# Second layer's entry: the low part of the first weight chunk on GpSimd, VectorE's context additions behind the first modulation

## The chip, the cores and the metric

The kernel runs on one core of a Trainium2 chip, as one program that holds two layers of a network. The metric is the time of one execution in microseconds of the device, taken over several runs. The engines are TensorE (PE in the profile; its weight loads are PEld), VectorE (DVE), ScalarE (ACT), GpSimd (POOL) and SyncE (SP), which issues most of the loads.

## What is computed

256 latent tokens and 256 context tokens, each of width 1024, pass through two layers. The part of a layer that matters here is its entry:

```python
for l in range(DEPTH):
    hx = modulate(rmsnorm(x_lat, norm1_g[l]), sh1[:, None], sc1[:, None])
    hc = modulate(rmsnorm(x_ctx, norm1_g[l]), csh1, csc1)
    mix_x, mix_c = token_mixer(hx, hc, tabs, p, lam, lam_init, not last)   # begins with hx @ w_in[l]
    x_lat = x_lat + g1[:, None] * mix_x
    hx2 = modulate(rmsnorm(x_lat, norm2_g[l]), sh2[:, None], sc2[:, None])
    x_lat = x_lat + g2[:, None] * ec_moe(hx2, router_w[l], moe_w1[l], moe_w3[l], moe_w2[l])
    ...                                   # the same for x_ctx where the layer isn't the last
return rmsnorm(x_lat, final_g)
```

`token_mixer` projects the tokens by `w_in` and runs four mixers; `compute_lambda` gives the two exponentials of `diff_lambda` that the second mixer needs. `ec_moe` is a mixture of 16 experts. All is float32.

## The kernel before

**How the engines are ordered.** Each engine has its own program, written out by hand, and runs it strictly in order; semaphores join them. A `Signal` is a semaphore with a count for each layer, and `wait_ge(*signal.at(l, n))` waits for the n-th event of layer l. An instruction that waits holds all that stands behind it on its engine.

**Weight chunks.** `w_in` comes in chunks of 128 x 1024 through a ring of six slots in SBUF. TensorE multiplies in a rounded form of float32, three products for one: high weights by high tokens, high by low, low by high. So each chunk j needs two steps before TensorE can use it: `high(l, j)` on ScalarE (line 1768) rounds the slot into `wr[:, j % 2, 0]` and raises `w_hi`; `low(l, j)` on VectorE (line 2250) subtracts that from the slot into `wr[:, j % 2, 1]` and raises `w_lo`. The slot is then free for SyncE's next load, which waits for `w_lo`. `high` of chunk j, from the third on, also waits for `chunk_sum` of chunk j - 2, since `wr` holds two chunks. In the first layer four opening chunks have their low parts made by GpSimd (line 2170).

**The entry of the second layer.** The last pack of the first layer's experts ends with eight products on TensorE, one for each half row tile of `x`. `add_last` on VectorE (line 2386) adds each to `x`: four for the latent tokens, then four for the context tokens. ScalarE takes squares of the latent tiles (lines 1775, 1785, 1788), VectorE their means (lines 2332, 2336, 2341), GpSimd the inverse roots (`roots`, line 2139). `normalise` on VectorE (line 2347) scales the two latent tiles, TensorE turns them (lines 1146 and 1162), and `modulate(l, 4)` makes four parts of modulated tokens: parts 0 and 2 by ScalarE (line 1818), 1 and 3 by VectorE (line 2365). Each part is then rounded by ScalarE (`part_high`, line 1807, signal `h_hi`) and its low part is made by VectorE (`part_low`, line 2353, signal `h_lo`). VectorE's order is part 1, low 0, part 3, low 1, low 2, low 3. ScalarE's is part 0, high 0, part 2, high 1, high 2, high 3, and then `high(l, 1)`. The first two projection chunks feed the branch `su`; TensorE's first chunk waits for `w_lo` 1 and then, for every two of its eight row blocks, for one more `h_lo`. A chunk of the first kind is 24 matmuls of 256 columns.

**Behind it.** VectorE then multiplies and sums `diff_lambda` (lines 2454 and 2455, signal `lam_step`). ScalarE waits for that (line 1873, one exponential) and only behind it, in its program, stand `high(l, 2)`, a square of a context tile, the first `su` output (line 1900, a Gelu), `high(l, 3)` and so on. The tables of Exp and Gelu are loaded in between. GpSimd's program has `roots(2 * l, 0, 1)`, both halves of the norm (latent, then context), then the load of the position bias (`load_bias`).

Of the kernel before, what the change touches and what calls it, by code (L numbers as in the profile page):

```python
# [288 lines left out]
def build(nc, A, out):  # L289
    f32, f32r = mybir.dt.float32, mybir.dt.float32r  # L290
    ACT = mybir.ActivationFunctionType
    ALU = mybir.AluOpType
# [4 lines left out]
    with ctx:  # L297
        def sb(name, shape, dt=f32, where=ctx):
            return where.enter_context(nc.sbuf_tensor(name, shape, dt))

        def signal(name, *per_layer):
            return Signal(ctx.enter_context(nc.semaphore(name)), list(per_layer))
# [6 lines left out]
        ring = ring_par[:, 0:NSLOT * 1024].rearrange("p (a b) -> p a b", a=NSLOT)  # L309
# [31 lines left out]
        with ExitStack() as mixers:  # L341
            wr = sb("wr", [128, 2, 2, 1024], f32r, mixers)
# [178 lines left out]
        def norm_pair(nn, j):  # L521

            a, b = tile_order(nn)[2 * j:2 * j + 2]
            return slice(a, b + 1, b - a)

        NN = [2 * n for _, _, n in norms]
        sq_done = signal("sq_done", *NN)
        sq_half = signal("sq_half", 1, 1)
        mean_done = signal("mean_done", norms[0][2], 0, norms[2][2], 0, 2)
        rstd_done = signal("rstd_done", *[n for _, _, n in norms[:4]], 2)  # L530
        xn_ready = signal("xn_ready", *NN)
        xt_ready = signal("xt_ready", 8, 8)
# [5 lines left out]
        w_hi = signal("w_hi", NC_ALL, NC_ALL)  # L538
        w_lo = signal("w_lo", NC_ALL, NC_ALL)
# [4 lines left out]
        aux_sum = signal("aux_sum", *[sum(u["kind"] in AUX for u in us) for us, _ in WU])  # L544
        tile_sum = signal("tile_sum", *[max(u.get("sums", 0) for u in us) for us, _ in WU])
        w_act = signal("w_act", *[n["act"] for _, n in WU])
        w_dve = signal("w_dve", *[n["dve"] for _, n in WU])
        dve_step = counter("dve_step")
# [160 lines left out]
        items, item_at = [], {}  # L709
# [102 lines left out]
        def last_bank(j, h, s):  # L812

            return 2 * j + h if s == 0 else (6, 7, 4, 5)[2 * j + h]
# [1302 lines left out]
        def _(pool):  # L2117
# [8 lines left out]
            def load_bias(l):  # L2126

                pool.dma_start(nab_all[:, :], A["na_rpb"][l]).then_inc(bias_loaded, 16)
# [6 lines left out]
            def roots(nn, *which):  # L2135
                for s in which:
                    pool.wait_ge(*mean_done.at(nn, s + 1))
                    c = norm_pair(nn, s)
                    pool.tensor_tensor(rstd[:, c], ms[:, c], half[:, 0:2], ALU.pow).then_inc(rstd_done.sem, 1)
# [14 lines left out]
            for l in range(L):  # L2154
# [9 lines left out]
                if l == 0:  # L2164
                    roots(2 * l, 0, 1)
                    for i in range(OPEN):
                        slot, _ = item_at["open_w", 0, i]
                        cols_ = slice(i % 2 * 512, i % 2 * 512 + 512)
                        pool.wait_ge(*w_hi.at(0, i + 1))
                        pool.tensor_tensor(wr[:, :, 1, cols_], ring[:, slot, :].rearrange("p (q n) -> p q n", q=2),  # L2170
                                           wr[:, :, 0, cols_].bitcast(f32), ALU.subtract).then_inc(w_lo.sem, 1)
                    pool.wait_ge(*mod_ready.at(0, 1))
                    load_bias(l)
                else:
                    roots(2 * l, 0, 1)
                    load_bias(l)

                pool.wait_ge(*v_stats.at(l, 1))
# [56 lines left out]
        def _(dve):  # L2235
            steps = [0]

            def step(ins):

                steps[0] += 1  # L2240
                ins.then_inc(dve_step, 1)
                dve.wait_ge(dve_step, steps[0])

            def low(l, j):

                if j >= NC_ALL or (l == 0 and j < OPEN):
                    return
                slot, _ = item_at["chunk", l, j]
                dve.wait_ge(*w_hi.at(l, j + 1))
                nc.vector.tensor_tensor(wr[:, j % 2, 1, :], ring[:, slot, :], wr[:, j % 2, 0, :].bitcast(f32),  # L2250
                                        ALU.subtract).then_inc(w_lo.sem, 1)

# [77 lines left out]
            def mean_half(nn, layer):  # L2330
                dve.wait_ge(*sq_half.at(layer, 1))
                step(nc.vector.tensor_scalar(ms_half, ss_half, 1.0 / D, EPS, ALU.mult, ALU.add))

            def mean_rest(nn):
                dve.wait_ge(*sq_done.at(nn, 2))
                nc.vector.scalar_tensor_tensor(out=ms[:, 1:2], in0=ss[:, 1:2], scalar=1.0 / D, in1=ms_half,
                                               op0=ALU.mult, op1=ALU.add).then_inc(mean_done.sem, 1)

            def mean_first(nn):
                dve.wait_ge(*sq_done.at(nn, 1))  # L2340
                return nc.vector.tensor_scalar(ms[:, 0:1], ss[:, 0:1], 1.0 / D, EPS, ALU.mult, ALU.add)

            def normalise(nn, s, which=(0, 1)):
                dve.wait_ge(*rstd_done.at(nn, s + 1))
                for j in which:
                    m = tile_order(nn)[2 * s + j]
                    nc.vector.tensor_scalar(xn[:, at_tile(m), :], x[:, m, :], rstd[:, m:m + 1], None, ALU.mult)\
                        .then_inc(xn_ready.sem, 1)
# [22 lines left out]
            def modulate(l, upto):  # L2371

                dve.wait_ge(*mod_ready.at(*MODULATED[l]))
                for t in range(1, upto, 2):
                    part_modulated(l, t)
                    if t > 1:
                        part_low(l, t - 2)
                    part_low(l, t - 1)
                part_low(l, upto - 1)

            def add_last(l, places):

                for s, j, h in places:
                    dve.wait_ge(*comb_sum.at(l, 2 * NT[l] * (NP[l] - 1) + 4 * j + 2 * h + s + 1))
                    xs_ = x[:, 2 * s + j, h * 512:(h + 1) * 512]
                    nc.vector.tensor_tensor(xs_, xs_, PS[:, last_bank(j, h, s), :], ALU.add).then_inc(comb_x.sem, 1)
# [46 lines left out]
            for l in range(L):  # L2433
# [3 lines left out]
                if l:  # L2437
                    add_last(l - 1, ((0, 0, 0), (0, 0, 1), (0, 1, 0), (0, 1, 1)))
                    step(mean_first(2 * l))
                    mean_half(2 * l, l - 1)  # L2440
                    mean_rest(2 * l)
                    add_last(l - 1, ((1, 0, 0),))
                    normalise(2 * l, 0)
                    add_last(l - 1, ((1, 0, 1), (1, 1, 0), (1, 1, 1)))
                if l:
                    low(l, 0)
                if l:
                    modulate(l, 4)
                    low(l, 1)

                dve.wait_ge(par_loaded[l], 16)
                lp = par[:, P_LAM:P_LAM + 256].rearrange("p (a b c) -> p a b c", a=2, b=2)
# [13 lines left out]
                for u in units:  # L2466
                    if splits_here(u):
                        low(l, u["q"] + 2)
                        if l:
                            context_step(l, u["q"])  # L2470
                        mod_work(l, PLAN_Q, u["q"])
                        for a, k in BY_Q[l].get(u["q"], ()):
                            accumulate(l, a, k)
# [463 lines left out]
```

## Time and profile before

| | |
|---|---|
| three runs | 1964.48, 1964.16, 1960.62 us; median 1964.16 |
| the profiled execution | 1961.55 us, of which the profile's span is 1959.7 us |
| TensorE busy | 1828.0 us (93%) |
| VectorE busy | 815.6 us (42%) |
| ScalarE busy | 454.2 us (23%) |
| GpSimd busy | 123.3 us (6%) |
| bytes read from HBM | 561.99 MB, 287 GB/s over the span |
| granted TensorE clock, mean | 0.989 of full speed |

All times in the trace count from the start of the span. The second layer's entry lies near 1100 us of it. "Idle before" is the time for which an engine had nothing to run before the instruction, and the arrow names what released it. Rows of a timeline merge neighbouring instructions of one line; the second number is then the time from the first one's start to the last one's end. Neighbouring instructions on VectorE and ScalarE overlap a little: the next one starts some 0.07 to 0.1 us before the row of the last one ends.

### The profile page before, as it was taken

Reading aid. Unit: us, or ns where it says so; the run is one execution under the profiler, and the core shown is the slowest. Engines: PE = TensorE matmul, PEld = TensorE weight load, DVE = VectorE, ACT = ScalarE, POOL = GpSimd, SP = SyncE. Lnnn points to the kernel's source line nnn. Section 1 sums busy time; section 2 is a strip of 40 time slices with the busy share of each in tenths; the row PEclk is TensorE's granted clock in tenths of the full one; section 3 lists DMA queues with packets and bytes.
Section 4 is the critical chain, followed back from the end, with each engine's and each line's share of the span. In section 5 each row is a group of like instructions: output and inputs, shape, how many; then the busy total and the mean of one; then the engine's idle time right before and its main releaser. Section 6 shows DMA issues by size and latency. Waiting matters only on the chain. (4 is left out here: it accounts for less than half of the span.)

```text
span 1959.7 us, 26828 instructions
## 1 busy us (share of the span) xinstructions
PE 1828.0 (93%) x11196; PEld 1092.6 (56%) x11196; DVE 815.6 (42%) x1242; ACT 454.2 (23%) x802; POOL 123.3 (6%) x137
## 2 busy tenths in 40 slices
PE   7999999999999999999888999999999988878786
PEld 5888766677888533333323587877997322222222
DVE  2676654665854422222211468667655010101001
ACT  3322244443222300000000342345443000000001
POOL 1081000000000100000000044000000000000000
PEclk8999999999999999999999999999999999999999
DMA  9635411113747999999999766643589999999997
GB/s 338 224 101 179 137 62 58 54 65 108 257 150 317 368 402 426 426 426 429 428 429 424 288 204 227 212 153 108 174 279 359 407 428 428 429 427 428 428 427 310
DMA packets 91985, 564.60 MB, mean 288 GB/s; under 512 B 10012, under 2 KB 10152, under 8 KB 67816
## 3 DMA queue, kind: packets, MB, share of 16 engines
q1 hardware_dynamic: 90824, 556.60, 72.6%
q0 software_dynamic: 512, 4.40, 0.6%
q10 hardware_dynamic: 544, 2.10, 0.3%
q8 instruction: 79, 1.29, 0.3%
q14 instruction: 26, 0.21, 0.0%
HBM read 561.99 MB, written 1.06 MB: 287 GB/s over the span
## 5 line engine op out<-in xcount | busy, mean ns | idle before, releaser
L1062 PE MATMUL PS<-hTr,wr 128*128 128x512 f32 (+1 forms) x2688 | 518.0, 349 | 8.4 <-DVE hTr L2353 5.7
L1062 PEld LDWEIGHTS PS<-hTr,wr 128*128 128x128 f32 x2688 | 428.3, 191 | 75.7 <-issue 15.2
L1644 PE MATMUL PS<-arena 128*32 128x512 f32 x1536 | 285.3, 603 | 45.8 <-DMA arena<-in_moe_w 22.5
L2250 DVE TENSOR_TENSOR wr<-ring_par,wr 128x1024 fp32r<-128x1024 f32 x148 | 186.9, 1263 | 134.0 <-ACT wr L1768 133.4
L1768 ACT ACTIVATE wr<-ring_par 128x1024 fp32r<-128x1024 f32 x148 | 156.4, 1057 | 269.5 <-PE PS L1062 265.1
L1644 PEld LDWEIGHTS PS<-arena 128*32 128x32 f32 x1536 | 81.8, 111 | 234.1 <-issue 234.1
L1062 PE MATMUL PS<-wr,hTr 128*128 128x512 f32 x816 | 188.8, 391 | 0.9 <-DVE wr L2250 0.9
L2794 DVE TENSOR_TENSOR x_work<-x_work,PS 128x512 f32<-128x512 f32 x72 | 45.7, 683 | 329.8 <-PE PS L1062 329.8
L1062 PEld LDWEIGHTS PS<-wr,hTr 128*128 128x128 f32 x816 | 151.9, 188 | 34.3 <-DVE wr L2250 2.3
L1644 PE MATMUL PS<-e_h,arena 128*32 128x512 f32 x720 | 121.6, 599 | 15.2 <-DMA e_h<-in_moe_w 15.0
L1644 PE MATMUL PS<-e_wr,arena 128*32 128x512 f32 x416 | 128.6, 602 | 0.4 <-PE PS L1644 0.4
L1644 PE MATMUL PS<-arena,nab 128*32 128x512 f32 x480 | 114.4, 601 | 9.7 <-DMA e_wr<-in_moe_w 6.7
L2076 ACT ACTIVATE arena<-PS 128x512 f32<-128x512 f32 x24 | 13.0, 594 | 413.1 <-PE PS L1644 413.0
L2822 DVE TENSOR_TENSOR nab<-PS,arena 128x512 f32<-128x512 f32 x24 | 15.5, 686 | 213.3 <-PE PS L1644 213.3
L1644 PE MATMUL PS<-e_h,nab 128*32 128x512 f32 x608 | 92.3, 593 | 4.4 <-DMA e_h<-in_moe_w 3.8
L1644 PEld LDWEIGHTS PS<-e_h,arena 128*32 128x32 f32 x720 | 35.9, 111 | 86.6 <-issue 86.6
L2271 DVE SCALAR_TENSOR_TENSOR spare<-ring_par,cond,spare 128x1024 f32<-128x1024 f32 x63 | 80.9, 1312 | 1.3
L2640 DVE SCALAR_TENSOR_TENSOR x_work<-x_work,PS 128x512 f32<-128x512 f32 (+1 forms) x56 | 32.1, 573 | 115.7 <-PE PS L1062 115.7
L1644 PEld LDWEIGHTS PS<-arena,nab 128*32 128x32 f32 x480 | 30.2, 111 | 79.3 <-issue 77.4
L1946 ACT ACTIVATE x_work<-PS,small 128x512 f32<-128x512 f32 (+1 forms) x96 | 58.2, 613 | 69.7 <-DVE small L2576 69.3
L1644 PE MATMUL PS<-e_wr,nab 128*32 128x512 f32 x256 | 74.2, 609 | 0.0
L2006 ACT ACTIVATE x_work<-PS 128x512 f32<-128x512 f32 (+1 forms) x64 | 31.4, 491 | 177.1 <-PE PS L1062 177.1
(250 smaller groups left out, 1938.2 us busy)
## 6 DMA issues: line engine op xcount, KB each, us to landing
arena<-in_moe_w SPq DMA_DIRECT2D x72, 2048.0 KB, 17.3
e_h<-in_moe_w SPq DMA_DIRECT2D x42, 2048.0 KB, 18.3
ring_par<-in_w_in SPq DMA_DIRECT2D x136, 512.0 KB, 3.7
e_wr<-in_moe_w SPq DMA_DIRECT2D x24, 2048.0 KB, 20.4
ring_par<-in_w_mod SPq DMA_DIRECT2D x92, 512.0 KB, 4.5
ring_par<-in_w_br SPq DMA_DIRECT2D x64, 256.0 KB, 3.5
e_h<-in_moe_w SPq DMA_DIRECT2D x32, 512.0 KB, 14.0
arena<-in_moe_w SPq DMA_DIRECT2D x32, 512.0 KB, 6.2
```

Of the source, the lines that this page charges most:

```text
L1062: return nc.tensor.matmul(o, a, b, start=first, stop=last)
L1644: ins = nc.tensor.matmul(PS[r:r + CAP, bank + h, :], src[:, k, r:r + CAP], rows_in(l, 6 * G * at_ + n + g, p, kk)[:, h * 512:(h + 1) * 512 ...
L1768: nc.scalar.activation(wr[:, j % 2, 0, :], ring[:, slot, :], ACT.Copy).then_inc(w_hi.sem, 1)
L1946: ins = nc.scalar.activation(p_t[:, i_ % 2, a, 0:nk], PS[:, a, 0:nk], ACT.Exp, bias=nmx[:, i_ % 2, a:a + 1], accum_out=rs[:, i_ % 2, a:a + 1])
L2006: nc.scalar.activation(sgt[:, n % 2, 0:tok], PS[:, 5, 0:tok], ACT.Tanh, scale=0.5)\
L2076: nc.scalar.activation(sil[:, h * 512:(h + 1) * 512], PS[:, h, :], ACT.Silu)\
L2250: nc.vector.tensor_tensor(wr[:, j % 2, 1, :], ring[:, slot, :], wr[:, j % 2, 0, :].bitcast(f32), ALU.subtract).then_inc(w_lo.sem, 1)
L2271: i = nc.vector.scalar_tensor_tensor(out=o, in0=ring[:, slot, :], scalar=c, in1=o, op0=ALU.mult, op1=ALU.add)
L2640: nc.vector.scalar_tensor_tensor(out=dst, in0=sgt[:, n % 2, 0:tok], scalar=1.0, in1=PS[:, 6, 0:tok], op0=ALU.add, op1=ALU.mult)\
L2794: nc.vector.tensor_tensor(xs_, xs_, PS[:, comb_bank(l, j, h) + s, :], ALU.add)\
L2822: nc.vector.tensor_tensor(ysb[:, h * 512:(h + 1) * 512], PS[:, 4 + h, :], g2r[:, h * 512:(h + 1) * 512], ALU.mult).then_inc(y_ready.sem, 1)
```

## The change

Three edits, all in the second layer's entry. GpSimd makes the low part of chunk 0 of the second layer, between the latent half and the context half of `roots`; VectorE's `low(l, 0)` is gone. VectorE's `low(l, 1)` waits for GpSimd's part, so that `w_lo` rises in order. The last three `add_last` additions, all to context tiles, move from ahead of `modulate(l, 4)` to behind `low(l, 1)`.

```diff
--- before.py
+++ after.py
@@ -2172,7 +2172,12 @@
                     pool.wait_ge(*mod_ready.at(0, 1))
                     load_bias(l)
                 else:
-                    roots(2 * l, 0, 1)
+                    roots(2 * l, 0)
+                    slot, _ = item_at["chunk", l, 0]
+                    pool.wait_ge(*w_hi.at(l, 1))
+                    pool.tensor_tensor(wr[:, 0, 1, :], ring[:, slot, :], wr[:, 0, 0, :].bitcast(f32), ALU.subtract)\
+                        .then_inc(w_lo.sem, 1)
+                    roots(2 * l, 1)
                     load_bias(l)
 
                 pool.wait_ge(*v_stats.at(l, 1))
@@ -2247,6 +2252,8 @@
                     return
                 slot, _ = item_at["chunk", l, j]
                 dve.wait_ge(*w_hi.at(l, j + 1))
+                if l and j == 1:
+                    dve.wait_ge(*w_lo.at(l, 1))
                 nc.vector.tensor_tensor(wr[:, j % 2, 1, :], ring[:, slot, :], wr[:, j % 2, 0, :].bitcast(f32),
                                         ALU.subtract).then_inc(w_lo.sem, 1)
 
@@ -2441,12 +2448,9 @@
                     mean_rest(2 * l)
                     add_last(l - 1, ((1, 0, 0),))
                     normalise(2 * l, 0)
-                    add_last(l - 1, ((1, 0, 1), (1, 1, 0), (1, 1, 1)))
-                if l:
-                    low(l, 0)
-                if l:
                     modulate(l, 4)
                     low(l, 1)
+                    add_last(l - 1, ((1, 0, 1), (1, 1, 0), (1, 1, 1)))
 
                 dve.wait_ge(par_loaded[l], 16)
                 lp = par[:, P_LAM:P_LAM + 256].rearrange("p (a b c) -> p a b c", a=2, b=2)
```

## Rows read from the trace of the kernel before

**Rows 1.** Chain that ended last: start us, us, what

```profile
1117.17 3.46 PE PS L1062 x18
...
1845.52 21.80 DMA arena<-in_moe_w
```

**Rows 2.** TensorE's timeline: start us, us, line, operation, tiles, count, [idle before]

```profile
1110.64 1.25 PE L1146 MATMUL PS<-cst,x_work 128*128 128x128 f32 x8
...
1115.76 10.62 PE L1062 MATMUL PS<-hTr,wr 128*128 128x256 f32 x72 [2.99 <-DVE hTr L2353]
1126.78 3.14 PE L1062 MATMUL PS<-hTr,wr 128*128 128x256 f32 x24 [0.40 <-DVE wr L2250]
```

**Rows 3.** Stretches: length, PE, PEld, DVE, ACT, POOL busy, clock, DMA, GB/s

```profile
1116.00:1118.00 2.00, 1.90 (x10) 1.60 (x10) 2.00 (x5) 1.65 (x3) 0.00 (x0) 0.53 0.53 207
```

**Rows 4.** VectorE's timeline at the second layer's entry

```profile
1109.77 1.42 DVE L2347 TENSOR_SCALAR x_work<-x_work,small 128x1024 f32<-128x1024 f32 x2 [0.23 <-POOL small L2139]
1111.10 1.88 DVE L2386 TENSOR_TENSOR x_work<-x_work,PS 128x512 f32<-128x512 f32 x3
1112.89 1.22 DVE L2250 TENSOR_TENSOR wr<-ring_par,wr 128x1024 fp32r<-128x1024 f32 x1
1114.02 0.99 DVE L2365 TENSOR_SCALAR arena<-PS,modA,modB 128x256 f32<-128x256 f32 x2
1114.93 0.68 DVE L2353 TENSOR_TENSOR hTr<-arena,hTr 128x512 fp32r<-128x512 f32 x1
...
1116.44 1.89 DVE L2353 TENSOR_TENSOR hTr<-arena,hTr 128x512 fp32r<-128x512 f32 x3
1118.24 1.22 DVE L2250 TENSOR_TENSOR wr<-ring_par,wr 128x1024 fp32r<-128x1024 f32 x1
...
1119.70 0.28 DVE L2455 TENSOR_REDUCE small<-modp 128x2 f32<-128x128 f32 x1
1120.25 0.16 DVE L2457 TENSOR_TENSOR small<-small 128x1 f32<-128x1 f32 x1 [0.27 <-ACT small L1873]
```

**Rows 5.** ScalarE's timeline at the second layer's entry

```profile
1108.75 1.06 ACT L1768 ACTIVATE wr<-ring_par 128x1024 fp32r<-128x1024 f32 x1
1111.77 1.02 ACT L1818 ACTIVATE arena<-PS,modB,modA 128x256 f32<-128x256 f32 x2 [1.96 <-PE PS L1146]
1112.82 0.63 ACT L1807 ACTIVATE hTr<-arena 128x512 fp32r<-128x512 f32 x1
1113.36 1.00 ACT L1818 ACTIVATE arena<-PS,modB,modA 128x256 f32<-128x256 f32 x2
...
1120.02 0.20 ACT L1873 ACTIVATE small<-small 128x2 f32<-128x2 f32 x1 [0.58 <-DVE small L2455]
1120.72 1.06 ACT L1768 ACTIVATE wr<-ring_par 128x1024 fp32r<-128x1024 f32 x1 [0.50 <-PE PS L1062]
...
1124.41 1.05 ACT L1768 ACTIVATE wr<-ring_par 128x1024 fp32r<-128x1024 f32 x1
```

**Rows 6.** Waits of ScalarE, 1100 to 1150: total us, times, longest

```profile
ACT wr L1768 <- PE PS L1062: 11.1, 8, 4.1
```

**Rows 7.** GpSimd's timeline: a low part in the opening, the roots

```profile
50.58 2.40 POOL L2170 TENSOR_TENSOR wr<-ring_par,wr 128x1024 fp32r<-128x1024 f32 x1 [6.01 <-ACT wr L1757]
...
1109.02 0.71 POOL L2139 TENSOR_TENSOR small<-small 128x2 f32<-128x2 f32 x1 [7.49 <-DVE small L2336]
```

**Rows 8.** Timelines of VectorE and GpSimd in other places

```profile
52.05 0.94 DVE L2457 TENSOR_TENSOR small<-small 128x1 f32<-128x1 f32 x1 [1.50 <-ACT small L1873]
...
1162.94 2.02 POOL L2200 TENSOR_SCALAR x_work<-x_work 128x240 f32<-128x240 f32 x1
...
1163.86 0.87 DVE L2269 TENSOR_SCALAR spare<-ring_par,cond 128x1024 f32<-128x1024 f32 x1
...
1169.06 1.66 DVE L2271 SCALAR_TENSOR_TENSOR spare<-ring_par,cond,spare 128x1024 f32<-128x1024 f32 x1
```

**Rows 9.** Costliest groups: names, shapes xcount, busy us, mean ns, idle before

```profile
L2271 DVE SCALAR_TENSOR_TENSOR spare<-ring_par,cond,spare 128x1024 f32<-128x1024 f32 x63 | 80.9, 1312 | 1.3
```

## The prediction

> **What bounds the kernel now.** I began with the page's chain that ended last, to see whether this entry lies on it at all. In order of time it runs through the weight products of both layers and then through the loads of expert weights: one piece is TensorE's first chunk of the second layer, a later one an expert load of 21.80 us [rows 1]. Nothing between the two has a fixed date of its own, so I take a shift of the entry to reach the end one to one.
>
> Next came TensorE's timeline there. It turns the latent tiles until about 1112.8, stands idle for 2.99 us until 1115.76, then runs three chunks of 24 matmuls, stands 0.40 us for a low part, and starts chunk 3 at 1126.78 [rows 2]. From there each chunk is paced by TensorE itself. So the date that counts is **the start of chunk 3**; whatever is gained in front of it is lost unless that date moves. The stretch view shows the price of the idle time: the granted clock is 0.53 in 1116 to 1118 [rows 3], the 1.2 GHz level, and 18 matmuls take 3.46 us, 192 ns each [rows 1], where at 2.4 GHz 24 take 3.14 us, 131 ns each or less [rows 2].
>
> VectorE's timeline shows what fills the idle 2.99 us: three context additions, 1111.10 to 1112.89, the low part of chunk 0, 1112.89 to 1114.02, and only then part 1 of the modulated tokens [rows 4]. That is 2.92 us of work ahead of the modulation. ScalarE's timeline shows what holds chunk 3. The exponential of lambda is at 1120.02, `high` of chunk 2 at 1120.72, released by TensorE's first chunk, and `high` of chunk 3 at 1124.41, because a square, a table load and a Gelu stand between the two [rows 5]. That ScalarE sequence of 3.69 us, then 1.05 for the rounding and 1.23 for the low part, is what chunk 3 waits for. ScalarE's rounding waits only for TensorE's sums, eight times, never for a load [rows 6].
>
> **The change, part by part.**
>
> *GpSimd's low part.* The operation is in the trace: 2.40 us for the same tile and size in the opening [rows 7]. GpSimd ends the roots at 1109.73 [rows 7]; the rounded weights are ready at 1109.81 [rows 5]. It can therefore start at about 1109.88, and alone would end at 1112.28. But VectorE's two normalisations run from 1109.77 to 1111.19 [rows 4]: two of 1024 elements in 1.42 us, against 1.22 for one subtraction of that size, so they take the fast form. Can the two engines run at once? In the opening, a VectorE operation of one element a partition started at 52.05, while GpSimd's low part ran from 50.58 to 52.98 [rows 7], and took 0.94 us to 52.99, where the same line takes 0.16 us here [rows 4, 8]. At 1162.94 a GpSimd instruction took 2.02 us, to 1164.96; inside it lies the whole of VectorE's 0.87 us fast scaling, to 1164.73 [rows 8]. So one blocks the other, and a waiting GpSimd instruction can be kept waiting by VectorE's next one. By this I let both normalisations pass and start GpSimd at 1111.2: it ends at **1113.6**. The bounds are 1112.28 (no blocking) and, if GpSimd got in first and VectorE waited, the second rival below.
>
> The Trainium skill (SBUF — State Buffer, section "Who interferes with whom") says that VectorE and GpSimd share one port pair, that whichever issues first keeps it for its whole instruction, and that a scaling in the two-port mode or a VectorE operation with two SBUF inputs contends with GpSimd. The trace agrees (0.94 us against 0.16). The page speaks against this change, since GpSimd's part is put right beside VectorE's normalisations; it leaves open who goes next after the first of them.
>
> *VectorE's modulation comes first.* After the normalisations it waits for the turned tiles, whose eight matmuls end at 1111.89 [rows 2]. Part 1 starts at 1111.95 instead of 1114.02 and takes 0.91 to the next start [rows 4]. Low 0 then needs ScalarE's `high` of part 0, which ends at 1113.45 whatever VectorE does [rows 5], and the port, free at 1113.6. So low 0 runs 1113.6 to 1114.25; before, 1114.93 to 1115.61 [rows 4]. Part 3 follows at 1114.2, low 1 at 1115.1 (ScalarE's part 2 ends at 1114.36 and a `high` takes 0.63, so 1114.95: in time [rows 5]), low 2 at 1115.7, low 3 at 1116.3 with steps of 0.60 [rows 4]. ScalarE has `high` of chunk 1 done near 1117.0 (three `high` of parts end near 1116.0, then 1.06), so `low(l, 1)` runs from 1117.0; before, 1118.24 [rows 4]. TensorE's first chunk starts at 1114.3, that is **1.45 us earlier**.
>
> *The additions behind it.* Three at 0.60 a step [rows 4] now stand between `low(l, 1)` and lambda. From the start of `low(l, 1)` to the end of the lambda sum took 1.74 us before (1118.24 to 1119.98) [rows 4]; now it takes 1.74 + 1.79 = 3.53. Starting at 1117.0, it ends at **1120.55**, 0.57 later than before. ScalarE's exponential needs that and its next `high` stands behind it. So: exponential 1120.59 to 1120.79, `high` of chunk 2 at 1120.81, against 1120.72 [rows 5]. The stall on TensorE's first chunk is gone, and the lambda stall is in its place. Everything behind is as before: `high` of chunk 3 at 1124.5, its low part done near 1126.8, chunk 3 on TensorE at 1126.87. Sum: **+0.1 us**. The 1.45 us won at the start become idle time between chunks. Chunk 1 can start at 1118.2 at the earliest; chunk 2 needs 1120.81 + 1.06 + 1.23 and two hand-overs of 0.04, so 1123.2, and then chunk 3 at 1126.87.
>
> *Costed at nothing.* The wait in `low(l, 1)` (GpSimd is done 3.4 us earlier). The context squares: the additions end at 1119.9, and the first square comes behind `high` of chunk 2, at 1121.8. The context half of the roots and the bias load, which stand behind the new instruction on GpSimd's queue: they come after 1129, and the new instruction is over by 1114. SyncE's next ring load waits for `w_lo`, released at 1113.6 by GpSimd where VectorE did it at 1114.11 [rows 4]; the loads are hidden, as the waits show [rows 6]. If they were not, the 0.5 us would be a gain.
>
> The profiled execution took 1961.55 us with a span of 1959.7, and so would take 1961.65. The median of the runs, 1964.16, lies 2.61 above it; 1964.16 + 0.1 gives **1964.3 us**. The three runs differ by 3.86 us, 0.2%, about what a measurement of this kernel can tell from no change.
>
> **The rivals.**
>
> *A. The clock falls a second time.* TensorE gets two new idle stretches, up to 2.2 us ahead of chunk 2 and 0.9 ahead of chunk 3. For it: 2.99 us of idle time was followed by 0.53 of the clock [rows 2, 3]. Against it: the first idle stretch shrinks to 1.5 us, and each new one is shorter than 2.99. Price: chunk 2 at 192 ns takes 4.6 us and ends at 1127.8, 0.9 late; chunk 3 at 192 instead of 131 ns adds 1.5. So +1.0 to +2.5, about 1966.
>
> *B. GpSimd gets in between the two normalisations (slower).* Then it runs 1110.5 to 1112.9 and the second normalisation follows, ending at 1113.6 instead of 1111.19: +2.4 us on the turned tiles, on every modulated part and, since the lambda path has no slack left, on chunk 3. It gives 1964.16 + 0.1 + 2.4 = 1966.7. For it: a VectorE operation at 1169.06 took 1.66 us, where its group's mean is 1.31, so there VectorE was made to wait although it had run just before [rows 8, 9]. Against it: the wait at 1162.94. It decides from the moment at which the second normalisation starts later than 1110.6. Only with A on top, about +4.9, does it pass 0.2%.
>
> *C. The whole gain arrives.* If lambda's sum came before 1119.3, for example because the additions ran in VectorE's waits, `high` of chunk 2 would follow TensorE's first chunk and chunk 3 would come up to 1.45 us earlier: 1962.7. Against it: VectorE runs in order, and the additions stand ahead of lambda.
>
> **How the numbers follow.** Forecast 0.55, A 0.17, B 0.18 (0.03 of it with A), C 0.07, something unseen 0.03. Without noise that is a spread from -1.5 to +2.5 about the forecast, that is 1962.8 to 1966.8; the runs' own scatter, which reaches 3.5 below their median, takes the range to 1960.3 to 1967.6. All cases but B with A lie inside 0.2% (3.9 us). Adding the scatter's tails and the unseen: faster 0.04, same 0.88, slower 0.08.
>
> **What the changed profile would show.** GpSimd's low part beginning near 1109.9 with a duration of 3.5 to 3.8 us, ending near 1113.6 (B: near 1112.9, with one normalisation of some 3 us). TensorE's first chunk near 1114.3. The exponential of lambda at about 1120.6 with ScalarE waiting for VectorE ahead of it, and `high` of chunk 2 released by nothing of TensorE. A TensorE idle time of 1 to 2 us ahead of chunk 2, released by VectorE's low part, and chunk 3 within 0.3 us of 1126.8. The prediction is wrong if chunk 3 starts more than 1 us off that, or if chunk 3 is on time and the end is not, which would mean that the entry does not reach the end one to one.

## The result, and the profile after

The changed kernel takes **1965.74 us** (median of 14 runs, 1962.9 to 1969.15) against 1963.19 us before (14 runs, 1960.15 to 1964.48): a ratio of 1.0016, 95% interval 1.0009 to 1.0024, some 3 us slower. The forecast was 1964.3 us and most likely within 0.2%. The range and the bound of 0.2% held, but the entry did not take the course that the forecast was built on; it took that of rival B. Forecast was a change of +0.1 us; measured is one of some 3 us.

All clock times below count from the start of each trace's span. Since the first layer ends up to 3.4 us apart in traces of one and the same code there, I compare from the first `add_last` of the entry: 1104.58 in the trace of before, 1106.09 in that of the changed kernel.

GpSimd's timeline of the changed kernel, the roots and the new low part:

```profile
1110.53 0.71 POOL L2139 TENSOR_TENSOR small<-small 128x2 f32<-128x2 f32 x1 [6.69 <-DVE small L2343]
1111.40 2.83 POOL L2178 TENSOR_TENSOR wr<-ring_par,wr 128x1024 fp32r<-128x1024 f32 x1 [0.16 <-ACT wr L1768]
```

VectorE's timeline of the changed kernel, the same stretch:

```profile
1111.28 3.50 DVE L2354 TENSOR_SCALAR x_work<-x_work,small 128x1024 f32<-128x1024 f32 x2 [0.23 <-POOL small L2139]
1115.60 0.99 DVE L2372 TENSOR_SCALAR arena<-PS,modA,modB 128x256 f32<-128x256 f32 x2 [0.82 <-PE PS L1146]
1117.08 0.69 DVE L2360 TENSOR_TENSOR hTr<-arena,hTr 128x512 fp32r<-128x512 f32 x1 [0.49 <-ACT hTr L1807]
...
1120.50 1.23 DVE L2257 TENSOR_TENSOR wr<-ring_par,wr 128x1024 fp32r<-128x1024 f32 x1
1121.64 1.88 DVE L2393 TENSOR_TENSOR x_work<-x_work,PS 128x512 f32<-128x512 f32 x3
...
1123.76 0.28 DVE L2459 TENSOR_REDUCE small<-modp 128x2 f32<-128x128 f32 x1
```

The two normalisations by their line (least, median and longest ns, first and last start):

```profile
L2354 DVE TENSOR_SCALAR x_work<-x_work,small x2: 754/1794/2835, 1111.3 to 1111.9; 128x1024 f32<-128x1024 f32 x2
```

GpSimd's low part was issued at 1111.40, while the first normalisation (from 1111.28, 0.75 us) ran. It took 2.83 us instead of 2.40. I read this as a wait until the first one had ended, at 1112.03, and then the port for GpSimd until 1114.23. The second normalisation was issued at about 1111.9 and took 2.84 us, until 1114.78. The pair takes 3.50 us where it took 1.42 [rows 4].

ScalarE's timeline of the changed kernel:

```profile
1115.37 1.02 ACT L1818 ACTIVATE arena<-PS,modB,modA 128x256 f32<-128x256 f32 x2 [4.05 <-PE PS L1146]
...
1124.08 0.20 ACT L1873 ACTIVATE small<-small 128x2 f32<-128x2 f32 x1 [2.30 <-DVE small L2459]
1124.18 1.04 ACT L1768 ACTIVATE wr<-ring_par 128x1024 fp32r<-128x1024 f32 x1
...
1127.86 1.05 ACT L1768 ACTIVATE wr<-ring_par 128x1024 fp32r<-128x1024 f32 x1
```

TensorE's timeline of the changed kernel:

```profile
1114.84 0.66 PE L1146 MATMUL PS<-cst,x_work 128*128 128x128 f32 x4 [2.09 <-DVE x_work L2354]
...
1117.92 0.94 PE L1062 MATMUL PS<-hTr,wr 128*128 128x256 f32 x6 [1.56 <-DVE hTr L2360]
1119.34 5.58 PE L1062 MATMUL PS<-hTr,wr 128*128 128x256 f32 x42 [0.47 <-DVE hTr L2360]
1126.61 3.14 PE L1062 MATMUL PS<-hTr,wr 128*128 128x256 f32 x24 [1.70 <-DVE wr L2257]
1130.22 3.14 PE L1062 MATMUL PS<-hTr,wr 128*128 128x256 f32 x24 [0.47 <-DVE wr L2257]
```

TensorE waits 2.09 us for the second normalisation in the middle of the first eight turning matmuls. Its first chunk starts 11.83 us after the first addition; before, 11.18 [rows 2]. ScalarE waits 2.30 us for lambda, and its next `high` follows at once: the stall that the forecast saw in place of the removed one is there. Chunk 2 comes after 1.70 us of idle time, and chunk 3 at 24.13 us after the first addition, against 22.20 before: **+1.93 us**.

The granted clock is the one thing that went better. Stretches of the changed kernel (length, busy us of PE, PEld, DVE, ACT and POOL, clock, DMA, GB/s):

```profile
1116.00:1118.00 2.00, 0.44 (x5) 0.23 (x4) 1.51 (x4) 1.97 (x5) 0.00 (x0) 1.00 0.54 217
...
1126.00:1128.00 2.00, 1.39 (x11) 1.39 (x12) 0.55 (x1) 1.97 (x5) 0.00 (x0) 1.00 0.23 18
```

It stays at 2.4 GHz through idle times of 2.09, 1.56 and 1.70 us; before, it fell behind 2.99 us [rows 2, 3]. That gains nothing, since chunk 0 isn't what ScalarE waits for.

The trace of the changed kernel is 7.6 us longer (1967.3 against 1959.7). By the dates of the two traces, 1.51 of that lie ahead of the first addition, in code that was not changed; 1.93 in the entry; 3.28 between chunk 4 and the first product of the modulation sums, a stretch called the pooling stage below; and 0.88 behind that. So the entry explains less than half of what that one pair of traces shows, and the pooling stage had to be explained too.

### The profile page after: what moved, and what is told of

It reads as the page before. It is cut to its first block and busy times, and to the rows that moved or that the text cites. A ratio compares the mean times of both kernels' runs of the same rounds, so it can differ in the third digit from the quotient of the medians.

```text
span 1967.3 us, 26829 instructions
## 1 busy us (share of the span) xinstructions
PE 1832.7 (93%) x11196; PEld 1093.0 (56%) x11196; DVE 818.0 (42%) x1241; ACT 454.0 (23%) x802; POOL 124.1 (6%) x138
## 5 line engine op out<-in xcount | busy, mean ns | idle before, releaser
L1644 PE MATMUL PS<-e_wr,nab 128*32 128x512 f32 x256 | 74.2, 608 | 0.0
```

The lines of the kernel that those rows point to most:

```text
L1644: ins = nc.tensor.matmul(PS[r:r + CAP, bank + h, :], src[:, k, r:r + CAP], rows_in(l, 6 * G * at_ + n + g, p, kk)[:, h * 512:(h + 1) * 512 ...
```

## The experiments

The columns: from the first addition to the first matmul of chunk 4, the first chunk of 512 columns (chunk 3 lies 2.98 us ahead of it in both traces above); the pooling stage, from there to the first product of the modulation sums (line 1115); the ratio to the kernel before by all runs.

| version | entry, us | pooling stage, us | ratio (95%) |
|---|---|---|---|
| before, three traces | 25.18, 25.38, 25.21 | 72.51, 72.48, 75.70 | 1.0001 (0.9993 to 1.0010) |
| changed, three traces | 27.11, 27.10, 27.11 | 75.79, 75.82, 74.16 | 1.0016 (1.0009 to 1.0024), 1.0013 (1.0004 to 1.0022) |
| GpSimd's part behind the normalisations | 25.02 | 72.49 | 1.0000 (0.9991 to 1.0009) |
| additions moved alone | 25.01 | 74.17 | 0.9993 (0.9984 to 1.0002) |
| GpSimd's part alone | 26.28 | 75.72 | 1.0004 (0.9994 to 1.0013) |
| lambda first, low part on VectorE | 24.06 | 75.78 | 0.9992 (0.9984 to 1.0001) |
| lambda first, low part on GpSimd | 24.27 | 72.49 | 0.9999 (0.9990 to 1.0008) |
| before, masks late | 25.26 | 71.34 | 0.9986 (0.9977 to 0.9995) |
| changed, masks late | 27.11 | 71.35 | 0.9997 (0.9988 to 1.0006) |
| lambda first on VectorE, masks late | 23.90 | 71.30 | 0.9984 (0.9975 to 0.9993) |

The stretch behind needs no column: from the modulation sums to the end all fourteen traces take 756.4 to 758.3 us, with no order by version.

**The two kernels again, three traces each.** No edit.

> The kernel before, unchanged, to see how much of a difference between two traces is one execution's scatter. From the first addition of the second layer's entry to chunk 3's first matmul the trace of before has 22.20 us and the trace of the changed kernel 24.13; from there to the start of the last long run of weight products 279.5 against 283.4 us. Theory (the collision of GpSimd's low part with the two normalisations, then a second loss in the pooling stage that follows from the shift): 22.2 and about 279.5 again. Rival (the later 4 us are an execution's scatter): 22.2, and the second figure anywhere between 279 and 284. Ratio 1.000 by both.

> The changed kernel, unchanged, profiled a second time. Theory: the two normalisations again take about 3.5 us together with GpSimd's low part between them, 24.1 us to chunk 3, and about 283 us from there. Rival (the order in which the port is granted is a matter of chance): 22.3 us to chunk 3 in this execution. Rival for the later part (scatter): 24.1, then a figure unlike 283. Ratio 1.0016 as before.

> The kernel before, profiled a third time. Theory (which engine gets the port at one place of the pooling stage is decided by some tens of ns, anew in each execution): 72.5 us in that stage again or 74.2 to 75.8. Rival (it is fixed by the kernel): 72.5.

> The changed kernel, profiled a third time. The entry: 24.1 us to chunk 3 again, with 3.5 us for the two normalisations, if the grant of the port there is fixed by the order of starts; 22.3 if it is chance. The pooling stage: theory (decided anew in each execution, in both kernels) 72.5 us is possible; rival (the change makes the slower course more likely, or certain) 74.2 to 75.8 a third time.

The entry repeats to 0.2 us in each kernel. (Where two ratios stand in the table, they are of two comparisons.) The normalisations took 3.50 us in all three traces of the changed kernel: at that place the grant of the port is not chance. The pooling stage does vary, and in the unchanged kernel as well: 72.5, 72.5 and 75.7 us. The rival "fixed by the kernel" falls; whether the change makes the long courses more frequent (three of three against one of three) is not settled by so few.

**GpSimd's part kept out of the normalisations.**

```diff
                     pool.wait_ge(*w_hi.at(l, 1))
+                    pool.wait_ge(*xn_ready.at(2 * l, 2))
                     pool.tensor_tensor(wr[:, 0, 1, :], ring[:, slot, :], ...)
```

> The changed kernel, with GpSimd's low part also waiting for the second normalisation (a wait on its signal added), so that it cannot run between the two. Theory, the collision costs the time: the normalisations take 1.42 us again, the low part runs about 2.4 us right behind them, TensorE's first chunk comes about 1.4 us earlier than before, and chunk 3 is at 22.3 us, held by lambda; ratio 1.0000 to 1.0005. Rival, the additions in front of lambda or something else in the change cost the time by themselves: chunk 3 stays at 24 us and the ratio at 1.0016.

GpSimd's timeline in this version, the low part:

```profile
1112.17 2.36 POOL L2179 TENSOR_TENSOR wr<-ring_par,wr 128x1024 fp32r<-128x1024 f32 x1 [1.60 <-DVE x_work L2355]
```

VectorE's, the normalisations and the sum of lambda:

```profile
1110.61 1.42 DVE L2355 TENSOR_SCALAR x_work<-x_work,small 128x1024 f32<-128x1024 f32 x2 [0.24 <-POOL small L2139]
...
1121.00 0.29 DVE L2460 TENSOR_REDUCE small<-modp 128x2 f32<-128x128 f32 x1
```

ScalarE's, lambda and the `high` of chunk 2:

```profile
1121.32 0.20 ACT L1873 ACTIVATE small<-small 128x2 f32<-128x2 f32 x1 [2.31 <-DVE small L2460]
1121.43 1.04 ACT L1768 ACTIVATE wr<-ring_par 128x1024 fp32r<-128x1024 f32 x1
```

TensorE's, chunks 0, 2 and 3:

```profile
1115.22 0.94 PE L1062 MATMUL PS<-hTr,wr 128*128 128x256 f32 x6 [1.61 <-DVE hTr L2361]
1116.64 6.73 PE L1062 MATMUL PS<-hTr,wr 128*128 128x256 f32 x42 [0.47 <-DVE hTr L2361]
1123.85 3.13 PE L1062 MATMUL PS<-hTr,wr 128*128 128x256 f32 x24 [0.49 <-DVE wr L2258]
1127.47 3.14 PE L1062 MATMUL PS<-hTr,wr 128*128 128x256 f32 x24 [0.49 <-DVE wr L2258]
```

One wait gives back all of it: the pair of normalisations takes 1.42 us, the low part 2.36, and from the first addition at 1105.42 chunk 3 is 22.05 us away, against 24.13. The collision is the cost in the entry. What remains is the forecast's own course, and no gain: TensorE starts 9.80 us after the first addition instead of 11.18, but of these 1.38 us 0.15 are left at chunk 3. It stands idle for 0.47 us in chunk 0 and for 0.49 us ahead of chunks 2 and 3, whose weights come late because ScalarE waits 2.31 us for lambda. And its clock fell behind the first idle stretch, of 1.61 us:

```profile
1118.00:1120.00 2.00, 2.00 (x12) 2.00 (x11) 2.00 (x3) 1.01 (x1) 0.00 (x0) 0.51 0.01 2
```

**Each half alone.** First the additions alone (the low part of chunk 0 on VectorE, right behind the normalisations), then GpSimd's part alone:

```diff
                     normalise(2 * l, 0)
-                    add_last(l - 1, ((1, 0, 1), (1, 1, 0), (1, 1, 1)))
-                if l:
                     low(l, 0)
-                if l:
                     modulate(l, 4)
                     low(l, 1)
+                    add_last(l - 1, ((1, 0, 1), (1, 1, 0), (1, 1, 1)))
```

> Only the second half of the change: the three context additions stand behind the low part of chunk 1; the low part of chunk 0 stays on VectorE, right behind the normalisations. Theory (collision is the cost, lambda holds ScalarE otherwise): TensorE's first chunk 1.4 us earlier, lambda's sum 0.5 us later, chunk 3 at 22.3 us, ratio 1.0000 to 1.0005. Rival (the moved additions are the cost): chunk 3 at 24 us, ratio 1.0016.

```diff
                     normalise(2 * l, 0)
+                    add_last(l - 1, ((1, 0, 1), (1, 1, 0), (1, 1, 1)))
                     modulate(l, 4)
                     low(l, 1)
-                    add_last(l - 1, ((1, 0, 1), (1, 1, 0), (1, 1, 1)))
```

(This second diff is against the changed kernel.)

> Only the first half of the change: GpSimd makes the low part of chunk 0, the additions stay ahead of the modulation. Theory: the normalisations take 3.5 us again; of the 2.1 us lost, the 1.13 us of the low part that VectorE no longer does come back, so chunk 3 is at 23.1 to 23.2 us, ratio 1.0005 to 1.0012. Rival (no collision without the moved additions): chunk 3 at 21.1 us, ratio 0.9995.

The moved additions cost nothing: 25.01 us, chunk 3 at 22.04; the ratio is even below what was expected, with 1.0000 inside its interval. GpSimd's part alone has the collision again, VectorE's line for it being this:

```profile
1109.10 3.50 DVE L2354 TENSOR_SCALAR x_work<-x_work,small 128x1024 f32<-128x1024 f32 x2 [0.23 <-POOL small L2139]
1112.53 1.87 DVE L2393 TENSOR_TENSOR x_work<-x_work,PS 128x512 f32<-128x512 f32 x3
```

It costs 1.1 us here (26.28 against 25.18), not 1.9; chunk 3 is at 23.30, a little beyond the 23.1 to 23.2 expected, and the ratio, 1.0004, a little below its range. It loses the same 2.08 us at the normalisations, but in this order the 1.13 us of the low part that left VectorE come back, ahead of the modulation and so ahead of lambda too. In the changed kernel VectorE spends them, and more, waiting for the turned tiles and for ScalarE (0.82 and 0.49 us).

**Lambda ahead of the additions.** VectorE keeps the low part; the three additions go behind the two lambda instructions. The second version is the one with the added wait on GpSimd, and the same move. The diff is against the version with the additions moved alone for the first, and against the one with the added wait for the second; the first lines show the additions leave, the last ones where they go.

```diff
                     modulate(l, 4)
                     low(l, 1)
-                    add_last(l - 1, ((1, 0, 1), (1, 1, 0), (1, 1, 1)))
...
                 nc.vector.reduce_sum(lam[:, 0:2], lt, axis=AX.X).then_inc(lam_step.sem, 1)
+                if l:
+                    add_last(l - 1, ((1, 0, 1), (1, 1, 0), (1, 1, 1)))
```

> Nothing on GpSimd; VectorE makes the low part of chunk 0 right behind the normalisations, while it would wait for the turned tiles, then the modulation and the low part of chunk 1, then the two lambda instructions, and only then the three context additions. Theory (no collision, and lambda's sum no longer behind the additions): the exponential of lambda is 1.2 us earlier than before, chunk 3 at 20.5 to 20.8 us, 1.4 to 1.7 less than before; ratio 0.9992. Rival (ScalarE's chain is held by something else, the additions' squares or TensorE's first chunk): chunk 3 at 22.2, ratio 1.0000.

> The change with both mends: GpSimd's low part waits for the second normalisation, and the additions stand behind the two lambda instructions. Theory: as with VectorE making that low part, chunk 3 at 20.5 to 20.9 us, ratio 0.9992; TensorE's first chunk is held until GpSimd's 2.4 us end. Rival (GpSimd's 2.4 us against VectorE's 1.2 show): 0.5 us or more later than the version with VectorE.

ScalarE's timeline in the first of the two (first addition at 1104.30):

```profile
1118.41 0.20 ACT L1873 ACTIVATE small<-small 128x2 f32<-128x2 f32 x1 [0.51 <-DVE small L2452]
1119.34 1.06 ACT L1768 ACTIVATE wr<-ring_par 128x1024 fp32r<-128x1024 f32 x1 [0.72 <-PE PS L1062]
```

Lambda is now 14.11 us behind the first addition, 1.33 earlier than before, and ScalarE's `high` of chunk 2 is again released by TensorE's first chunk, 15.04 us behind it where it was 16.14. So chunk 3 gains 1.1 us on before, and 0.96 on the additions moved alone (22.05 against 21.09), from which this version differs only in lambda's place: this is what rival C needed, and it shows that lambda's place kept most of the gain away. The expectation of 1.4 to 1.7 was too high. The clock fell here behind 1.56 us of idle time and kept TensorE's first chunk long, which now is what ScalarE waits for (0.72 us); TensorE's row and the stretches show it:

```profile
1114.06 0.94 PE L1062 MATMUL PS<-hTr,wr 128*128 128x256 f32 x6 [1.56 <-DVE hTr L2353]
...
1114.00:1116.00 2.00, 1.47 (x8) 1.30 (x9) 2.00 (x5) 2.00 (x5) 0.00 (x0) 0.79 0.48 188
1116.00:1118.00 2.00, 2.00 (x12) 2.00 (x11) 1.99 (x4) 1.88 (x2) 0.00 (x0) 0.50 0.00 0
```

GpSimd's slower low part costs 0.05 us at TensorE's first chunk (9.81 against 9.76). Its chunk 3 is at 21.29 against 21.09, which also misses the expected 20.5 to 20.9, and its ratio is 0.9999 where 0.9992 was expected. The same order with the low part on VectorE and the masks late has 20.91, so 0.2 us either way is within what the fall and rise of the clock make of the first chunk.

**Where the pooling stage forks.** Two traces of the *unchanged* kernel, the first and the third, at the same place of its program (line 2485 is a multiplication of two SBUF tensors, line 2250 the low part of a chunk; up to here the two traces agree to 0.1 us in every VectorE and GpSimd instruction behind chunk 4). VectorE's timeline in the first:

```profile
1178.05 0.69 DVE L2485 TENSOR_TENSOR x_work<-x_work,cst 128x512 f32<-128x512 f32 x1
...
1194.62 1.92 DVE L2250 TENSOR_TENSOR wr<-ring_par,wr 128x1024 fp32r<-128x1024 f32 x1
```

VectorE's in the third:

```profile
1177.64 1.16 DVE L2485 TENSOR_TENSOR x_work<-x_work,cst 128x512 f32<-128x512 f32 x1
...
1187.40 1.93 DVE L2250 TENSOR_TENSOR wr<-ring_par,wr 128x1024 fp32r<-128x1024 f32 x1
```

GpSimd's timeline in the first (line 2196 is the pooling's running sum, line 2212 the eight mask additions):

```profile
1175.76 4.62 POOL L2196 TENSOR_TENSOR x_work<-x_work 128x271 f32<-128x271 f32 x4
...
1185.03 12.38 POOL L2212 TENSOR_TENSOR nab<-nab,cst 128x384 f32<-128x384 f32 x8
```

GpSimd's in the third:

```profile
1175.34 4.07 POOL L2196 TENSOR_TENSOR x_work<-x_work 128x271 f32<-128x271 f32 x4
...
1182.09 12.90 POOL L2212 TENSOR_TENSOR nab<-nab,cst 128x384 f32<-128x384 f32 x8
```

In the first trace VectorE's multiplication goes first and takes 0.69 us, and GpSimd's sums take 4.62. In the third GpSimd goes first: 1.16 and 4.07. From there the two engines meet in another order; GpSimd reaches its masks at 78.0 us behind the first addition instead of 80.45, and they lie on other low parts. TensorE's timeline in the first trace of before:

```profile
1196.59 5.75 PE L1062 MATMUL PS<-wr,hTr 128*128 128x512 f32 x24 [0.86 <-DVE wr L2250]
```

TensorE's in the third trace of before:

```profile
1197.83 7.24 PE L1062 MATMUL PS<-wr,hTr 128*128 128x512 f32 x24 [2.36 <-DVE wr L2250]
```

TensorE's in the third trace of the changed kernel:

```profile
1199.80 5.76 PE L1062 MATMUL PS<-wr,hTr 128*128 128x512 f32 x24 [2.36 <-DVE wr L2257]
```

It waits 0.86 us for a low part, or 2.36; and behind the same 2.36 us of idle time the chunk takes 7.24 us in one of these two traces and 5.76 in the other. The clock fell behind that wait in the first of the two only. Stretches of the third trace of before:

```profile
1198.00:1200.00 2.00, 2.00 (x5) 1.61 (x6) 1.90 (x2) 0.00 (x0) 0.00 (x0) 0.50 0.41 111
1200.00:1202.00 2.00, 2.00 (x8) 1.53 (x8) 2.00 (x3) 0.00 (x0) 0.00 (x0) 0.73 0.95 356
```

Stretches of the third trace of the changed kernel, the same place:

```profile
1200.00:1202.00 2.00, 2.00 (x10) 1.60 (x10) 1.90 (x2) 0.00 (x0) 0.00 (x0) 1.00 0.63 123
```

That makes three lengths of the stage, and the eleven traces with the masks in their old place all fit: 72.5 where VectorE's multiplication went first (four), 74.2 where GpSimd went first and the clock stayed up (two), 75.7 to 75.8 where it fell (five).

To take the fork out, the masks are held back until the projections of keys and values are summed:

```diff
                 pool.wait_ge(bias_loaded, 16 * (l + 1))
+                if l:
+                    pool.wait_ge(*chunk_sum.at(l, KV_CHUNKS))
```

> The kernel before, with GpSimd's eight additions of the neighbourhood mask (second layer) held back until the projections of keys and values are summed, so that they no longer run beside VectorE in the pooling stage. From the start of the first wide chunk to the first product of the modulation sums, traces so far show 72.5 us (TensorE waits 0.86 us for a low part), 74.2 or 75.8 (it waits 2.34 us, with or without a fall of the clock behind). Theory (those masks, beside VectorE, cause both): 71.7 us, no wait above 0.3 us. Rival (the pooling operations in front of the masks are enough to cause it): 72.5 or more. Ratio 0.9990 to 0.9998 by the theory.

> The changed kernel with the same holding back of the masks. Theory (the change itself costs only what the entry shows, the rest is the fork in the pooling stage): 24.1 us to chunk 3, then the same 71.7 us as its partner, so that its ratio lies 0.0010 above that of its partner, 1.9 us. Rival (the change makes the pooling stage slower by its own doing): 2 us or more above 71.7, and a ratio 0.0016 or more above its partner's.

> VectorE's low part of chunk 0 behind the normalisations, lambda ahead of the three additions, and the masks held back. Theory: 21.1 us to chunk 3, then 71.7 us; 1.2 us less than the kernel before with the masks held back, and 2 us less than the kernel before; ratio 0.9985 to 0.9992. Rival (gains of the entry are lost again behind it): the ratio of the kernel before with the masks held back.

TensorE in the kernel before with the masks late:

```profile
1186.50 16.58 PE L1062 MATMUL PS<-wr,hTr 128*128 128x512 f32 x72
```

All 72 matmuls run without a wait, and the stage takes 71.34, 71.35 and 71.30 us in the three versions (71.7 was expected, and a ratio of 0.9990 or more for the first). The grant still went either way in these traces. VectorE's multiplication in the kernel before with the masks late:

```profile
1179.97 1.17 DVE L2487 TENSOR_TENSOR x_work<-x_work,cst 128x512 f32<-128x512 f32 x1
```

VectorE's in the changed kernel with the masks late:

```profile
1182.74 0.69 DVE L2491 TENSOR_TENSOR x_work<-x_work,cst 128x512 f32<-128x512 f32 x1
```

So the wait came from those masks beside VectorE, and without them the order of the grants ahead of them has no effect. The second line also shows that the changed kernel, whose code is the same up to this place, can take VectorE's turn first: the long course is not certain in it. With the stage equal, the changed kernel is 1.85 us behind its partner by the traces (27.11 against 25.26), and 0.0011, some 2.2 us, by the ratios.

## Why the prediction was right and wrong

*The number.* 1965.74 us lies inside the range of 1960.3 to 1967.6 because the range is 7.3 us wide and was drawn to take in rival B; the course given 0.55 did not happen. The prediction's own sign of being wrong was met: chunk 3 at 24.13 us where 22.3 was forecast, more than 1 us off. The lower bound doesn't follow from the numbers given for it either (1962.8 less 3.5 is 1959.3), and for the upper one none is given. And the median of three runs on which the forecast was built, 1964.16, lies 1 us above that of fourteen, 1963.19, which by luck brought the forecast nearer to what was measured.

*The place that counts.* Right: what is lost or won at chunk 3 reaches the end. With the masks late, the 1.85 us between the two kernels at chunk 4 are still 1.86 at the modulation sums (98.46 against 96.60 us from the first addition), and the stretches behind, 757.8 and 757.9 us, don't take them back.

*GpSimd's low part.* Its price was right (2.36 us alone). The step that failed is the next one: "By this I let both normalisations pass and start GpSimd at 1111.2". That rested on one row of a waiting GpSimd instruction, and in the normalisations GpSimd got in after the first one, in all five traces in which it was free to. With one added wait that keeps it behind both, chunk 3 is back at 22.05 us. This was rival B, given 0.18. B's price was +2.4 on the second normalisation and +2.5 at chunk 3; measured were 2.08 and 1.93. The first was overstated by 0.32: GpSimd held VectorE for 2.20 us and not 2.40 (from 1112.03 to 1114.23; it had spent the rest while it waited), and the second normalisation ended 0.55 us behind GpSimd, where it ends 0.67 behind the first one in the kernel before (1.42 less 0.75). The second is less again because lambda came only 0.47 us later behind the normalisations (forecast 0.57), and ScalarE's next `high` starts 0.10 us behind it, not 0.22.

*Modulation first, lambda later.* Right, and shown where the collision is absent: TensorE's first chunk 1.38 us earlier (forecast 1.45), lambda 0.46 later (0.57), chunk 3 within 0.15 us of before (forecast +0.1), ratio 1.0000. In the changed kernel the wait for lambda, 2.30 us on ScalarE, is there as well.

*What was costed at nothing* stayed at nothing: the wait in `low(l, 1)`, the context squares, GpSimd's later roots and the ring loads show in no wait of the entry.

*Rival A.* The clock did not fall in the changed kernel's entry, although idle times of 1.6 to 2.1 us were there. It fell later, in the pooling stage, in traces of both kernels. The argument against it, that the first idle stretch shrinks to 1.5 us, does not hold on the forecast's own course: behind 1.56 us (additions moved alone) and 1.61 us (GpSimd's part behind the normalisations) the clock fell to 0.50 and 0.51. It cost nothing at chunk 3, since lambda held ScalarE.

*Rival C.* It did not happen in the change, for the reason given against it. Put in another order it is real: 1.1 us at chunk 3.

*What was not foreseen.* A stage of the unchanged kernel, 70 us behind the edit, takes one of three lengths that differ by up to 3.3 us. It has a part in the scatter of the runs, which the prediction took as given, but how large a part is open: the standard deviation of the runs is 1.5 us for the kernel before and still 1.2, 1.2 and 0.8 us for the three versions with the masks late, in the same comparison. Of the 2.6 to 3.1 us by which the changed kernel is slower, 1.9 are shown to be the collision: they are in all its traces and go with one wait. The rest is inside the intervals; whether it is a more frequent long course of the pooling stage stays open (by the grant, GpSimd went first in three of four traces of the changed kernel and in two of four of the kernel before, those with the masks late counted in).

The best version here is the kernel before with the masks late and lambda ahead of the additions: 1960.29 us against 1963.44 in the same comparison, ratio 0.9984. Most of that is the masks'; the 1.4 us that lambda's place adds in the entry (23.90 against 25.26) are seen in the trace and not resolved by the ratios (0.9984 and 0.9986).

## What to carry to other kernels

Before work goes to GpSimd, look at what VectorE runs in those very microseconds: the second of two back-to-back scalings from SBUF to SBUF can be held for nearly the whole of GpSimd's instruction (2.84 us instead of 0.75 here), so give GpSimd's part a wait behind them. Follow the freed engine's program to the next thing that another engine waits for (here a two-number exponential), since that is where a reordering is paid. And where two engines contend for one port over many instructions, profile the unchanged kernel more than once: a difference between two single traces may be a fork that both kernels have.

## What was not expected of the hardware

- Which engine is granted the port next is not one rule. A GpSimd subtraction that arrived 0.12 us behind the start of the first of two scalings was let in between them, five times of five; in [rows 8] a waiting GpSimd scaling of 240 elements let VectorE's fast scaling pass to its end first. In the pooling stage one such grant went either way in traces of the same kernel, and there the starts tell which way: in all fourteen traces GpSimd's sum went first where it had started 7 to 26 ns ahead of VectorE's multiplication (nine traces), and VectorE's went first where the two started within 5 ns of each other (five).
- A GpSimd instruction that waits for the port does part of its work meanwhile: 2.83 us from issue to end, of which about 0.6 us is waiting by my reading, against 2.36 alone.
- The clock fell behind 2.36 us of idle time in one trace and not in another with the same work around it (7.24 us against 5.76 for 24 matmuls of 512 columns); it fell behind 1.56 us in the version with lambda first and in that with the additions moved alone, and stayed up behind 2.09, 1.56 and 1.70 us in the changed kernel.
